# A hybrid decoder trunk layer on one core: five 128-row expert tiles as split weights, the fourth up piece split earlier, the last token tile's residual in halves

## What is computed

```python
x = x + concatenate([conv_out, gla_out]) @ w_out[l]
hf = rmsnorm(x, ffn_norm_g[l])
x = x + hier_moe(hf, ...)          # router: top-1 of 4 groups, top-2 of its 8 experts
return rmsnorm(x, final_norm_g)
...
def expert_block(args):
    xblk, e = args
    return (jax.nn.silu(xblk @ w_gate[e]) * (xblk @ w_up[e])) @ w_down[e]
```

## Time and profile before

| | |
|---|---|
| median of three runs | 1027.51 us |
| profiled execution | 1031.98 us, of which the span is 1030.2 us |
| PE busy | 977.8 us (95%) |
| DVE, ACT, POOL busy | 571.0, 388.3, 331.6 us |
| matmuls | 4485 |
| mean granted share of TensorE's clock | 0.98 |
| DMA | 264.96 MB, mean 257 GB/s |
| chain that ended last | PE 75%, DMA 12%, DVE 5%, ACT 3% |

### The profile page before, as it was taken

The page is one execution under the profiler, slowest core; times in us unless marked ns, Lnnn a source line. Parts: engine busy times, 40 slices in busy tenths (PEclk is TensorE's granted clock), DMA queues, the critical chain, the costliest instruction groups (busy, mean ns, idle before and its releaser), DMA issues.

```text
span 1030.2 us, 11923 instructions
## 1 busy us (share of the span) xinstructions
PE 977.8 (95%) x4485; PEld 658.2 (64%) x4485; DVE 571.0 (55%) x706; ACT 388.3 (38%) x515; POOL 331.6 (32%) x245
## 2 busy tenths in 40 slices
PE   6999999999999999999999999899999999999991
PEld 5748888888778888754545553566643456755560
DVE  5468999978787667843123312334310058841765
ACT  6567357343473221332132112224211056631652
POOL 0275998952230000212121311132221215622133
PEclk9989999999999999999999999999999999999996
DMA  9620202020072353789999999999999999999984
GB/s 317 188 83 1 82 1 81 1 82 2 1 266 82 124 204 112 272 301 348 392 386 366 368 418 404 355 360 407 335 356 372 397 404 402 358 388 386 392 301 192
DMA packets 65293, 264.96 MB, mean 257 GB/s; under 512 B 10853, under 2 KB 29477, under 8 KB 40656
## 3 DMA queue, kind: packets, MB, share of 16 engines
q1 hardware_dynamic: 51792, 237.07, 58.9%
q0 software_dynamic: 10032, 18.60, 7.3%
q10 hardware_dynamic: 3408, 8.48, 2.1%
HBM read 249.44 MB, written 28.84 MB: 270 GB/s over the span
## 4 chain that ended last, share of the span: by engine, by line
PE 75%; DMA 12%; DVE 5%; ACT 3%; issue 2%; SPq 1%; POOL 1%; POOLq 0%; ACTq 0%; DVEq 0%
PE ps L2274 15%; PE ps L2288 6%; PE ps L2246 5%; PE ps L2248 5%; PE ps L2247 5%; PE ps L1998 4%; PE ps L2000 4%; PE ps L1999 4%; PE ps L2105 3%; PE ps L2107 3%; PE ps L2106 3%; DMA raw_b<-in_expert_w_gate_dram 3%; DMA summed_rows<-ym,idx_g 2%; PE ps L2239 2%; DMA raw<-in_expert_w_up_dram 2%
## 5 line engine op out<-in xcount | busy, mean ns | idle before, releaser
L2274 PE MATMUL ps<-raw_b,xm 128*64 128x512 f32 (+1 forms) x384 | 167.3, 593 | 0.2 <-ACT xm L1242 0.2
L2274 PE MATMUL ps<-raw,xm 128*64 128x512 f32 (+1 forms) x320 | 139.6, 594 | 0.0
L857 POOL DMA_INDIRECT summed_rows<-ym,idx_g x25 | 49.6, 1982 | 176.7 <-DVE ym L1819 176.7
L842 POOL DMA_INDIRECT xg<-hf_rows,idx_g x27 | 37.1, 1376 | 194.2 <-PE ps L2239 171.3
L2274 PEld LDWEIGHTS ps<-raw_b,xm 128*64 128x64 f32 (+1 forms) x384 | 58.4, 155 | 64.1 <-issue 63.6
L1393 DVE SCALAR_TENSOR_TENSOR ps<-uT,pcol,ps 128x1024 f32<-128x1024 f32 (+1 forms) x87 | 96.5, 1109 | 2.4
L2246 PE MATMUL ps<-hi_a,xm_hi 128*128 128x512 f32 x208 | 85.6, 412 | 12.0 <-DVE lo_a L1777 5.8
L768 POOL TENSOR_TENSOR acc<-x,acc 128x1024 f32<-128x1024 f32 x30 | 85.2, 2841 | 31.4 <-ACT x L1028 27.3
L1777 DVE TENSOR_TENSOR lo_a<-raw,hi_a 128x2048 fp32r<-128x2048 f32 x24 | 54.6, 2287 | 65.3 <-ACT hi_a L1225 65.3
L1802 DVE TENSOR_TENSOR hm<-sg,ps 128x512 f32<-128x512 f32 x27 | 29.6, 1097 | 109.8 <-PE ps L2274 86.8
L2248 PE MATMUL ps<-hi_a,xm_lo 128*128 128x512 f32 x208 | 85.1, 409 | 0.0
(11 more groups left out here) (363 smaller groups left out, 2171.8 us busy)
## 6 DMA issues: line engine op xcount, KB each, us to landing
raw_b<-in_expert_w_gate_dram SPq DMA_DIRECT2D x32, 1024.0 KB
raw_b<-in_expert_w_up_dram SPq DMA_DIRECT2D x32, 1024.0 KB, 11.0
raw_b<-in_expert_w_down_dram SPq DMA_DIRECT2D x32, 1024.0 KB, 12.0
raw<-in_expert_w_up_dram SPq DMA_DIRECT2D x32, 1024.0 KB
raw<-in_expert_w_gate_dram SPq DMA_DIRECT2D x32, 1024.0 KB, 10.4
raw<-in_expert_w_down_dram SPq DMA_DIRECT2D x32, 1024.0 KB, 8.0
raw<-in_w_in_dram SPq DMA_DIRECT2D x8, 1024.0 KB, 6.4
xa<-in_x_dram SPq DMA_DIRECT2D x8, 512.0 KB, 9.2
```

The costliest lines, as they stand in the source:

```text
L857: return pool.indirect_dma_start(out=sum_dram, out_offset=bass.IndirectOffsetOnAxis(ap=at.bitcast(U32), axis=0), in_=src, in_offset=None, ...
L2274: last = pe.matmul(ps[r * m:(r + 1) * m, i // 2, :], xm[:, kk, r * m:(r + 1) * m], slot(n, i)[:, w], start=(kk == 0), stop=(kk == KC - 1))
```

## The change

Five tiles, 3, 8, 16, 18 and 24, go from N to S; each of them stands right behind a pair. The first tile stays N. The kind H and its tile `xm_head` are new in the code, but no letter of the string is an H. The planner works with other kinds, but its list of loads comes out the same: SP issues the same transfers in the same order.

```diff
-    KINDS = "NSPNPDEPNPDEPDEPNPNSSSSPNST"
+    KINDS = "NSPSPDEPSPDEPDEPSPSSSSSPSST"
...
-            sp.wait_ge(x2_rdy, NT)
+            sp.wait_ge(x2_rdy, NT + 1)
...
-            for t in range(NT):
+            for t in range(NT - 1):
                 row_rms(t)
+            a, b = stat[:, 48:49], stat[:, 24 + NT - 1:24 + NT]
+            pool.wait_ge(ss_rdy, 2 * NT + 1)
+            pool.tensor_tensor(b, a, b, ALU.add).then_inc(last_sum, 1)
+            pool.wait_ge(last_sum, 1)
+            row_rms(NT - 1)
+            pool.wait_ge(gf_in, 16)
+            pool.wait_ge(hn_rdy, 1)
+            v = hfp[:, (NT - 1) % 2, :].rearrange("p (j q) -> p j q", j=KC)
+            pool.tensor_tensor(v, v, g_ffn[:].rearrange("p (q j) -> p j q", j=KC), ALU.mult).then_inc(hf_rdy, 1)
...
+            def last_squares(half):
...
+            def last_rows_stored():
+                t = NT - 1
+                act.dma_start(sum_v[t], x2[:, t, :]).then_inc(sum_out[t // (NT // 2)], 16)
+                act.wait_ge(rs_rdy, t + 2)
+                act.activation(hfp[:, t % 2, :].rearrange("p (j q) -> p j q", j=KC),
+                               x2[:, t, :].rearrange("p (q j) -> p j q", j=KC), ACT.Copy,
+                               scale=stat[:, 40 + t:41 + t]).then_inc(hn_rdy, 1)
+                act.wait_ge(hf_rdy, t + 1)
+                act.dma_start(hf_v[t], hfp[:, t % 2, :]).then_inc(hf_out[t % 2], 16)
...
                     up_hi(t + 1, 2)
+                    if not first(t):
+                        up_hi(t + 1, 3)
...
                 if t:
                     rows_out(t - 1)
                 hidden_hi(t)
-                if more:
+                if first(t):
                     up_hi(t + 1, 3)
...
-            residual(NT - 1)
+            last_residual(1)
             place(NT - 2)
-            normed(NT - 1)
             choose(NT - 1)
...
-                    for i in (2,) if first(t) else (1, 2):
+                    for i in (2,) if first(t) else (1, 2, 3):
                         up_lo(t + 1, i)
                 if t:
                     rows_out(t - 1)
                 if hidden_split(t):
                     hidden_lo(t)
+                if first(t):
+                    up_lo(t + 1, 3)
                 if more:
-                    up_lo(t + 1, 3)
...
             def x2_transposed(t, half):
-                pe.wait_ge(x2_rdy, t + 1)
+                pe.wait_ge(x2_rdy, t + 1 + (half if t == NT - 1 else 0))
```

More of the change, by code:

```diff
@@ L246, in layer_program @@
         xm = at("xm", [P, KC, P], over=o_xm)
+        xm_head = at("xm_head", [P, 4, P], over=o_t + 14 * D)
         hmT = at("hmT", [P, FC, P], over=o_hm)
@@ L1243, in x_hi @@
                 else:
+                    if isinstance(t, int) and KINDS[t] == "H":
+                        act.activation(xm_head[:].rearrange("p j i -> p (j i)"), ps[:, 2, :], ACT.Copy).then_inc(xn_rdy, 1)
                     act.activation(xm_hi[:].rearrange("p j i -> p (j i)"), wide(2), ACT.Copy).then_inc(xh_rdy, 1)
@@ L1564, in residual, with last_residual @@
                 dve.tensor_tensor(x2[:, t, :], wide(2 * (t % 2)), xin[:, t % 2, :], ALU.add).then_inc(x2_rdy, 1)
+            def last_residual(half):
+                t, c = NT - 1, slice(half * 512, (half + 1) * 512)
+                if half:
+                    dve.wait_ge(yo_ps, NT)
+                else:
+                    dve.wait_ge(w_used, 1)
+                dve.wait_ge(x_in[t % 2], 16 * (t // 2 + 1))
+                dve.tensor_tensor(x2[:, t, c], ps[:, 2 * (t % 2) + half, :], xin[:, t % 2, c], ALU.add).then_inc(x2_rdy, 1)
             def normed(t):
@@ L2290, in down_native, with head_native @@
                 last.then_inc(split_used, 1)
+            def head_native(t):
+                n = tile_pos[t][0]
+                pe.wait_ge(xn_rdy, KINDS[:t + 1].count("H"))
+                pe.wait_ge(*slot_in(n, 0))
+                for k in range(4):
+                    last = pe.matmul(ps[:, 0, :], xm_head[:, k, :], slot(n, 0)[:, k * F:(k + 1) * F], start=(k == 0), stop=False)
+                last.then_inc(split_used, 1)
             def gate_up(t):
@@ L2300, in gate_up @@
                         pe.wait_ge(xl_rdy, 1)
+                    if KINDS[t] == "H" and i == 0:
+                        continue
                     if native:
```

22 lines of the change are left out of this document (18 added, 4 removed).

## The result

The changed kernel takes 1045.87 us, the median of four runs (1043.56 to 1048.42), where the kernel before takes 1027.29 on the same chip (1023.20 to 1035.67). The ratio is 1.0171, 95% interval 1.0103 to 1.0239: 18.6 us slower by the medians. The forecast was 1031 with a range to 1038.

What follows compares the result with a forecast made beforehand. Expert loads were taken to fill the DMA engines (share 0.98), so 18.9 us of PE savings count 0. The end moves +3.6, already holding -1.6 and +0.6: 1027.5 + 3.6 = 1031.1, say 1031; range 1017 to 1038.

Steps and rivals of the forecast that it cites:

- The bound: Expert loads from 438.9 to 988.4 us: DMA engines at share 0.98, so 18.9 us of saved PE time count 0.
- The estimate of 26 us: Five tiles going native to split: three passes in place of four save 5.2 us of PE a tile.
- the most that any speeding up of PE can win: Expert loads, 438.9 to 988.4 us: all unused DMA time is 2% of 549.5, 11 us, with the bytes unchanged.
- Fourth piece ahead of the leaving rows, middle: Tile 22: ACT's wait before the fourth piece goes and 1.6 us of unused DMA fills; -1.6, bounds -4 to 0.
- The splits' cost: Tiles 3, 8, 16, 18 and 24: no net time counted; tile 24 has bounds 0 to +3.6.
- DVE's 14.3 us a tile: Six added subtractions in each new split tile, at most 2.4 us each; DVE has room, so busy time costs nothing.
- The end: Tile 23's `ym` waits for tile 25's fourth piece, delaying scatters and the sums' load: +3.6, bounds 0 to +7.
- The last token tile: Before the first gather: normed rows stored later, after ACT's scaling and POOL's product; +0.6, bounds -1.7 to +1.7.
- its row: Store of normed rows at 420.45 us: read as moving nothing to land for 7.9 us beside 1 MB pieces.
- The split's latency starves the loads: Five split tiles: late fourth pieces free slots later and the load queue runs dry; 1038, up to 1042, chance 0.17.
- PE is the bound after all: Expert stages: earlier requests land earlier, so PE's savings count; 1006, or 1017 for half; chance 0.13 for both.
- the end's chain isn't delayed: Kernel's end: tile 25's piece lands early enough or scatters go quicker; -1.6 + 0.6 gives 1026.5, chance 0.25.

Runs made afterwards that it cites:

- the splits alone: The five added split tiles put into the kernel before, with its old order and the last residual in one piece: 1029.78 us, ratio 1.0012.
- third product out: The kernel before without the product of low rows and high weights in every split piece, so its output differs: 1010.54 us, ratio 0.9849.
- old order at tile 18: The whole change, but in tile 18's step the leaving rows of pair 17 go ahead of tile 19's fourth piece again: 1032.54 us, ratio 1.0039.
- the order alone: The kernel before with only the fourth piece moved ahead of the leaving rows, no added split tiles, residual in one piece: 1035.00 us, ratio 1.0057.
- splits and halves: The changed kernel with the leaving rows ahead of the fourth piece again, as in the kernel before: 1031.10 us, ratio 1.0026.
- the run above: The kernel before with the last token tile's residual in halves and the multiply by g_ffn on VectorE instead of GpSimd: 1028.28 us, ratio 1.0002.

## Why the prediction was right or wrong

**The bound: right, its ceiling wrong.** Tile 10's fourth piece landed at 652.97 (forecast 652, give or take 1), PE's busy time fell by 14.5 us (18.9 counted, "some 15 or more" as the sign), the waits for low parts passed 15, and the splits alone changed nothing. The estimate of 26 us by the four passes of the Trainium skill ("FP8 and Floating Point Precision", TensorE Precision Notes) is further from these 14.5. But the 11 us of unused DMA time were not "the most that any speeding up of PE can win": with the third product out the loads took 17.7 us less. A later PE costs, and an earlier one gains a little beyond the share.

**The failed step is the term "Fourth piece ahead of the leaving rows, middle", put at -1.6 with bounds of -4 to 0.** It read the place where the old order cost something, tile 22, and there it held: PE no longer waits there for a low part. But it did not follow the leaving rows where they now stood behind a late piece. At tile 18 these rows are a pair's: two serial scatters, then a gather on POOL's queue, and one buffer for `ym`. With the split tiles in place that one step measured some +13 us, give or take 7 (old order at tile 18: 1.0171 to 1.0039); in the trace it is the 8.5 us wait for tile 21's rows and the loads issued 9.0 us later. The same text did follow this chain for the end of the kernel, with `ym`, both scatters and what waits behind them. It was the same kind of place one stage earlier, and the forecast did not look through `KINDS` for other pairs whose rows now wait for a fourth piece two tiles on. Besides tile 23 there is one: 17 (behind the other pairs that place holds a pair, or an E, which loads nothing).

**The splits' cost was missed as an interaction.** Alone they cost 0, as forecast. Beside the new order the cost goes from some 6 us to 13 or 14; the intervals overlap, but PE's wait (2.7 and 7.7 us) and the distance of the two loads (9.4 and 17.1, before 7.8) say the same. Part of this shows in the POOL rows above: more subtractions on DVE go with longer indirect transfers on POOL (last section). The forecast counted DVE's 14.3 us a tile (74.2 us more in all, 571.0 to 645.2) as free because DVE has room. By these rows it is the placing of that time beside POOL that costs; no run moved the subtractions alone.

**The end: right, in its kind and about in its size.** +3.6 was forecast for a later `ym` of tile 23. In the changed kernel:

```profile
980.88 0.74 DVE L1865 TENSOR_SCALAR ym<-ps,gate_col 128x512 f32<-128x512 f32 x1
...
1007.25 3.78 SPq L684 DMA_DIRECT2D sums<-summed_rows  x8
```

`ym` stands behind a third low part (978.67), and the chain to the sums is 26.4 us long (25.7 in the earlier trace rows). The sums are loaded 3.9 us ahead of the end of tile 26's hidden transposes, where it was 8.5. The tail is 2.8 us longer, in the order alone 3.9.

**The last token tile: right sign, wrong cause, and small.** +0.6 was forecast from a late store of normed rows. The store landed early enough, 5.9 us from its issue at 418.35, and ACT's stores shared the engines with the loads while it did. The rule of the Trainium skill, "DMA: Bandwidth & Descriptors", Queues, rings and completion order, that an engine goes round-robin between queues was set aside by the forecast for its row; as far as these rows go, which show sharing and not its order, the traces agree with the rule. DMA queues in 418.3 to 426 us of the changed kernel (packets, MB, share of 16 engines; q10 also holds the end of the store of the residual rows):

```profile
q1 hardware_dynamic: 172, 1.15, 35.5%
q10 hardware_dynamic: 241, 0.86, 27.2%
...
hf_rows<-hfp ACTq DMA_DIRECT2D x1, 512.0 KB, 5.9
```

In the kernel before too, from 420.8 to 428 us, q10 had 32.0% of the engines beside q1's 65.5%. So the row was misread: the 7.9 us to landing did not mean that the store moved nothing. The cost, 2.3 us in the trace and 2.6 in the medians, was the mask held by POOL's multiply, which the forecast had priced by its own length alone.

**The rivals.** "The split's latency starves the loads" gave 1038 to 1042 at 0.17 and came nearest in size, partly by luck. Its last link happened (slots free too late, the engines short of loads at 893 to 907), but not by its first: splits and halves without the new order is at 1.0026. "PE is the bound after all" is ruled out by the splits alone (1.0012), "the end's chain isn't delayed" by the tail, 33.3 to 36.6 us with the new order against 30.8 before.

## What to carry to other kernels

When work is moved ahead of a step in an in-order queue, list every tile at which that happens, and for each follow the step that now waits through all queues behind it, down to the next thing that gathers or frees a buffer; the worst tile decides, not the one the change was made for. If one delayed event reaches the busy engine by two roads, cutting either shows nothing, so an experiment without effect doesn't clear its cause. Time on an engine that "has room" can cost when another engine's short instructions, which are on the path, get longer beside it. And before a gap is laid to a change, look for it in the kernel before: the 18.1 us without a load were there too.

## What was not expected of the hardware

**GpSimd's indirect transfers wait for VectorE's subtractions.** In all kernels profiled here, 546 indirect scatters began beside no `lo_a` or `lo_b` subtraction (two SBUF inputs of 128x2048) and took 1.46 to 1.71 us. 114 began inside a run of them; 80 of these took the rest of the run plus 1.5 us (within 0.15), the other 34 were let in at an earlier gap. The longest, in the kernel before:

```profile
879.62 10.02 POOL L857 DMA_INDIRECT summed_rows<-ym,idx_g  x1 [7.21 <-DVE ym L1819]
```

VectorE had subtractions up to 888.1, 8.5 us from its begin. The changed kernel's second scatter of the pair 17 took 5.98 us beside three subtractions that ended at 861.7, 4.5 us from its begin:

```profile
854.98 6.69 DVE L1823 TENSOR_TENSOR lo_b<-raw_b,hi_a 128x2048 fp32r<-128x2048 f32 x3
```

The run of the splits alone, whose expectation said this ahead, has a scatter of 5.61 us at 4.1 us of rest. That the subtractions are the cause rests on these lengths. No run moved them alone.

**It goes the other way too.** VectorE's mask of 0.24 us took 3.3 us in five kernels, where it waited for GpSimd's multiply and memset, 2.4 in three, where it got in between the two, and 0.24 with the multiply gone, which the run above showed. The Trainium skill, "SBUF — State Buffer", Who interferes with whom, says that a VectorE instruction in a two-port mode and a GpSimd instruction exclude each other for the whole instruction, and that one with two SBUF inputs contends with a GpSimd instruction that reads SBUF. The lengths of the mask agree with this if it runs in a two-port mode, which no row shows. For the scatters the same section infers the contrary, that `tensor_tensor` does not hold up the transfers that GpSimd issues; there the 80 lengths above differ from it, and they decide.
